# Undilated keys turned on VectorE instead of TensorE, with the pairs of that group moved later

## The reference

```python
for l in range(DEPTH):
    y = mixer_sublayer(x, ...)            # below
    x = layer_norm(alpha * x + y, ln_g[l], ln_b[l])

(aq, ak, av, ag, su, sv, sg, mq, mk, mv, mo, mg, mi, mf) = split_columns(x @ w_in)
aq = apply_partial_rope(aq, cos, sin); ak = apply_partial_rope(ak, cos, sin)
for gi, (window, dilation) in enumerate(ATT_GROUPS):   # (128, 1), (512, 4), (2048, 16)
    o, lse = dilated_window_attention(aq[gi], ak[gi], av[gi], window, dilation)
att = softmax over the groups' lse, applied to their o
...                                       # sgu, mLSTM with gates mi, mf
mix = concatenate([att * silu(ag), sgu * silu(sg), ml * silu(mg)])
return mix @ w_out
```

## Time and profile before

| | us |
|---|---|
| median of 3 runs | 1279.9 |
| the profiled execution, its own time | 1278.3 |
| its span, first to last instruction | 1276.6 |
| TensorE matmul busy | 1260.4 (99%) |
| VectorE busy | 896.2 (70%) |
| ScalarE busy | 694.4 (54%) |
| GpSimd busy | 248.0 (19%) |

### The profile page before, as it was taken

How to read it: one execution, slowest core, us unless ns; L and a number is a source line. 1 busy time by engine, 2 the same in 40 slices (tenths; PEclk the granted TensorE clock), 3 DMA queues, 4 the chain that set the end, 5 groups by cost and what they waited for, 6 DMA issues and landing times.

```text
span 1276.6 us, 16392 instructions
## 1 busy us (share of the span) xinstructions
PE 1260.4 (99%) x6358; PEld 1041.7 (82%) x6358; DVE 896.2 (70%) x1229; ACT 694.4 (54%) x959; POOL 248.0 (19%) x268
## 2 busy tenths in 40 slices
PE   9999999999999999999999999999999999999996
PEld 8888888888888888888888788887888888888885
DVE  5786876975667655865775769768756676567656
ACT  5477476555555544444564765666555655345441
POOL 0321522422320000400003223334131200004000
PEclk9999999999999999999999999999999999999998
DMA  9968758764665555466667587678546646555662
GB/s 334 316 200 262 235 189 271 263 200 140 204 200 171 188 185 183 155 224 194 201 199 224 190 271 232 210 251 278 184 133 217 191 153 214 165 188 198 190 208 89
DMA packets 129277, 264.97 MB, mean 208 GB/s; under 512 B 8824, under 2 KB 8976, under 8 KB 128688
## 3 DMA queue, kind: packets, MB, share of 16 engines
q1 hardware_dynamic: 123712, 247.23, 60.4%
q0 software_dynamic: 3680, 13.28, 3.0%
q10 hardware_dynamic: 1808, 3.42, 0.7%
HBM read 258.61 MB, written 5.28 MB: 207 GB/s over the span
## 4 chain that ended last, share of the span: by engine, by line
PE 92%; POOL 3%; DVE 2%; issue 2%; ACT 0%; DVEq 0%; POOLq 0%; ACTq 0%
PE ps L373 85%; PE ps L444 1%; PE ps L684 1%; DVE w_lo L1079 1%; DVE mix L1240 1%; PE ps L391 1%; PE ps L652 1%; POOL arena L1701 1%; PE ps L543 0%; POOL arena L1697 0%; PE ps L528 0%; PE ps L355 0%; PE ps L556 0%; POOL arena L1698 0%; PE ps L667 0%
## 5 line engine op out<-in xcount | busy, mean ns | idle before, releaser
L1079 DVE TENSOR_TENSOR w_lo<-w_raw,w_hi 128x1024 fp32r<-128x1024 f32 x408 | 529.3, 1315 | 321.2 <-ACT w_hi L749 319.8
L749 ACT ACTIVATE w_hi<-w_raw 128x1024 fp32r<-128x1024 f32 x408 | 428.3, 1058 | 404.2 <-PE ps L373 339.7
L373 PE MATMUL ps<-w_hi,xT_hi 128*128 128x512 f32 x1616 | 637.1, 394 | 4.5 <-DVE w_lo L1079 3.8
L373 PE MATMUL ps<-w_hi,xT_lo 128*128 128x512 f32 x1616 | 629.7, 390 | 0.0
L373 PE MATMUL ps<-w_lo,xT_hi 128*128 128x512 f32 x1616 | 629.2, 389 | 0.0
L373 PEld LDWEIGHTS ps<-w_hi,xT_hi 128*128 128x128 f32 x1616 | 303.4, 188 | 70.3 <-issue 7.4
L373 PEld LDWEIGHTS ps<-w_hi,xT_lo 128*128 128x128 f32 x1616 | 303.4, 188 | 63.9
L373 PEld LDWEIGHTS ps<-w_lo,xT_hi 128*128 128x128 f32 x1616 | 303.6, 188 | 61.2
L292 POOL TENSOR_TENSOR carried<-ident 1x1 f32<-1x1 f32 x30 | 17.6, 586 | 453.7 <-DVE arena L1433 178.7
L1240 DVE CUSTOM_DVE_ANT_0 mix<-xres,mix 128x1024 f32<-128x1024 f32 x64 | 88.4, 1381 | 1.1
L820 ACT ACTIVATE arena<-arena 32x256 f32<-32x256 f32 x128 | 53.2, 416 | 12.1 <-DVE arena L1156 10.5
(11 more groups left out here) (248 smaller groups left out, 847.2 us busy)
## 6 DMA issues: line engine op xcount, KB each, us to landing
w_raw<-w_in_dram SPq DMA_DIRECT2D x367, 512.0 KB, 4.5
w_raw<-w_out_dram SPq DMA_DIRECT2D x64, 512.0 KB, 4.8
mix<-gate_w_dram SPq DMA_DIRECT2D x32, 512.0 KB, 5.5
xres<-x_dram ACTq DMA_DIRECT2D x4, 512.0 KB, 8.9
v_dram<-arena POOLq DMA_DIRECT2D x4, 512.0 KB, 6.4
z<-v_dram POOLq DMA_DIRECT2D x8, 256.0 KB, 5.3
z<-ln_g_dram POOLq DMA_DIRECT2D x2, 1024.0 KB, 7.6
store<-ln_b_dram POOLq DMA_DIRECT2D x2, 1024.0 KB, 7.9
```

The source lines that it names most:

```text
L373: mm = pe.matmul(ps[2 * s + t][:], a[:, order[c] * KC + k, t * P:(t + 1) * P], b[:, k], start=(c + k + i == 0), stop=(c == CH - 1 and k == ...
L749: A(hi_of(n, c), w_raw[:, c % RING], ACT.Copy).then_inc(w_hi_done, 1)
L1079: TTn(lo_of(n, c), w_raw[:, c % RING], hi_of(n, c).bitcast(F32), ALU.subtract).then_inc(w_lo_done, 1)
```

## The change

The two copies `keys_copied` and TensorE's `key_transposes` go; the last group's keys take the path of the others, `turn(1)` on VectorE and `moved(1, ...)` on ScalarE. The scores of the first two pairs stand one chunk and a half or so later, behind the first chunk of the MO block instead of behind chunk 6 of the value block, and what follows them is moved likewise; the values of the last two pairs stand behind the first chunk of SU. On VectorE the gate pieces stand between remainders, in all three groups. The diff without the two removed copy functions and without the parts that only repeat such shifts:

```diff
 TensorE, last group
-                    def key_transposes():
-                        pe.wait_ge(roped, qk + 2)
-                        ...
-                                tr = pe.transpose(ps[6 + m // 2][:, at:at + P], z[:, 1, t, m * P:(m + 1) * P], ident[:])
-                        tr.then_inc(qk_ps, 1)
                     def scores(p):
                         if p == 0:
                             pe.wait_ge(qkT_act, qk + 2)
-                            pe.wait_ge(qkT_dve, l + 1)
+                            pe.wait_ge(comp_og_act, comp)
+                            pe.wait_ge(comp_og_dve, comp)
 ...
-                    chunks(n0 + 2, q0 + 2, 1, 0, 5)
-                    key_transposes()
-                    chunks(n0 + 2, q0 + 2, 1, 5, 7)
+                    chunks(n0 + 2, q0 + 2, 1, 0, CH)
+                    chunks(n0 + 3, q0 + 3, 0, 0, 1)
                     scores(0)
                     scores(1)
-                    chunks(n0 + 2, q0 + 2, 1, 7, 8)
-                    chunks(n0 + 3, q0 + 3, 0, 0, 1)
+                    chunks(n0 + 3, q0 + 3, 0, 1, 3)
                     prob_transposes(0)
-                    chunks(n0 + 3, q0 + 3, 0, 1, 2)
+                    chunks(n0 + 3, q0 + 3, 0, 3, 4)
                     prob_transposes(1)
-                    chunks(n0 + 3, q0 + 3, 0, 2, 3)
+                    chunks(n0 + 3, q0 + 3, 0, 4, 5)
 ...
                     for p in range(2):
                         values(p)
                     for p in range(2, PAIRS):
                         scores(p)
-                    chunks(n0 + 3, q0 + 3, 0, 3, 5)
+                    chunks(n0 + 3, q0 + 3, 0, 5, 7)
                     prob_transposes(2)
-                    chunks(n0 + 3, q0 + 3, 0, 5, 6)
+                    chunks(n0 + 3, q0 + 3, 0, 7, 8)
                     prob_transposes(3)
-                    chunks(n0 + 3, q0 + 3, 0, 6, 7)
-                    for p in range(2, PAIRS):
-                        values(p)
-                    chunks(n0 + 3, q0 + 3, 0, 7, 8)
 ...
-                chunks(N_SU, Q_SU, 0, 0, CH)
+                chunks(N_SU, Q_SU, 0, 0, 1)
+                for p in range(2, PAIRS):
+                    values(p)
+                chunks(N_SU, Q_SU, 0, 1, CH)
 ScalarE, last group
+                    split(n0 + 3, 0, 1)
+                    moved(1, 0, 8)
+                    split(n0 + 3, 1, 2)
+                    moved(1, 8, 16)
+                    split(n0 + 3, 2, 3)
 ...
-                    keys_copied()
-                    split(n0 + 3, 0, 3)
+                    take(n0 + 3, 1, vA[:, 0, :])
+                    split(n0 + 3, 3, 5)
                     exponentials(0)
-                    split(n0 + 3, 3, 4)
-                    take(n0 + 3, 1, vA[:, 0, :])
+                    split(n0 + 3, 5, 6)
                     exponentials(1)
                     prob_copy(0)
-                    split(n0 + 3, 4, 6)
+                    split(n0 + 3, 6, 8)
                     prob_copy(1)
 ...
                     prob_copy(2)
-                    split(n0 + 4, 0, 1)
+                    split(n0 + 4, 2, 3)
+                    take(N_SU, 0, mix[:, 0, 2 * BW:3 * BW])
                     prob_copy(3)
 VectorE, every group
-                    gate_sums(1)
-                    split(n0 + 2, 0, 4)
+                    split(n0 + 2, 0, 1)
+                    for i in pieces(g, 1):
+                        gate_piece_sums(i)
+                        c = i - pieces(g, 1)[0] + 1
+                        split(n0 + 2, c, c + 1)
+                    split(n0 + 2, 3, 4)
                     take(n0 + 2, 0, z[:, 1, 1, :])
-                    gate_sums(2)
-                    split(n0 + 2, 4, 8)
+                    for i in pieces(g, 2):
+                        gate_piece_sums(i)
+                        c = i - pieces(g, 2)[0] + 4
+                        split(n0 + 2, c, c + 1)
+                    split(n0 + 2, 6, 8)
+                    turn(1)
 VectorE, last group
-                    keys_copied()
-                    split(n0 + 3, 0, 2)
+                    split(n0 + 3, 0, 3)
                     ...
+                    take(n0 + 3, 1, vA[:, 1, :])
+                    split(n0 + 3, 3, 4)
                     score_maxima(0)
                     score_maxima(1)
 ...
                     prob_copy(2)
-                    split(n0 + 4, 0, 1)
+                    split(n0 + 4, 2, 3)
+                    take(N_SU, 0, mix[:, 1, 2 * BW:3 * BW])
                     prob_copy(3)
```

More of the change, by code:

```diff
@@ L811, in moved @@
                     def moved(which, first, last):
-                        act.wait_ge(turned, l * (2 * GROUPS - 1) + g * 2 + which + 1)
+                        act.wait_ge(turned, qk + which + 1)
                         for i in range(first, last):
@@ L891, in _ @@
                     split(n0 + 2, 4, 8)
-                    if g < NCOMP:
[L893 to L897, removed]
+                    split(n0 + 3, 0, 1)
[3 more added lines that the diff above has]
+                    split(n0 + 3, 2, 3)
+                    if g < NCOMP:
                         take(n0 + 3, 1, vS[:, 0])
@@ L906, in _ @@
                         continue
-                    keys_copied()
-                    split(n0 + 3, 0, 3)
+                    take(n0 + 3, 1, vA[:, 0, :])
+                    split(n0 + 3, 3, 5)
                     exponentials(0)
-                    split(n0 + 3, 3, 4)
-                    take(n0 + 3, 1, vA[:, 0, :])
+                    split(n0 + 3, 5, 6)
                     exponentials(1)
                     prob_copy(0)
-                    split(n0 + 3, 4, 6)
+                    split(n0 + 3, 6, 8)
                     prob_copy(1)
-                    split(n0 + 3, 6, 7)
+                    split(n0 + 4, 0, 1)
                     exponentials(2)
                     output_copy(0)
-                    split(n0 + 3, 7, 8)
                     exponentials(3)
                     output_copy(1)
+                    split(n0 + 4, 1, 2)
                     prob_copy(2)
-                    split(n0 + 4, 0, 1)
+                    split(n0 + 4, 2, 3)
+                    take(N_SU, 0, mix[:, 0, 2 * BW:3 * BW])
                     prob_copy(3)
-                    split(n0 + 4, 1, 3)
+                    split(n0 + 4, 3, 5)
                     output_copy(2)
                     output_copy(3)
-                    take(N_SU, 0, mix[:, 0, 2 * BW:3 * BW])
-                    split(n0 + 4, 3, 5)
                     act.wait_ge(mdiff_done, l * GROUPS + g + 1)
@@ L1158, in turn @@
                         f.then_inc(turned, 1)
-                    def keys_copied():
-                        dve.wait_ge(qk_ps, l + 1)
-                        V.tensor_copy(kT[:, 2:4, :], ps[7][:].rearrange("p (m t) -> p m t", m=2)).then_inc(qkT_dve, 1)
                     def comp_maxima():
@@ L1303, in _ @@
                     turn(0)
-                    gate_sums(1)
-                    split(n0 + 2, 0, 4)
-                    take(n0 + 2, 0, z[:, 1, 1, :])
-                    gate_sums(2)
-                    split(n0 + 2, 4, 8)
+                    split(n0 + 2, 0, 1)
[4 more added lines that the diff above has]
+                    split(n0 + 2, 3, 4)
+                    take(n0 + 2, 0, z[:, 1, 1, :])
+                    for i in pieces(g, 2):
[4 more added lines that the diff above has]
+                    turn(1)
                     if g < NCOMP:
-                        turn(1)
                         split(n0 + 3, 0, 3)
@@ L1325, in _ @@
                         TTn(gate_sum[:], gate_acc[:, :, 0, :], gate_acc[:, :, 1, :], ALU.add).then_inc(gates_summed, 1)
+                    take(n0 + 3, 1, vA[:, 1, :])
+                    split(n0 + 3, 3, 4)
                     score_maxima(0)
                     score_maxima(1)
-                    split(n0 + 3, 2, 4)
-                    take(n0 + 3, 1, vA[:, 1, :])
+                    split(n0 + 3, 4, 6)
                     prob_copy(0)
-                    split(n0 + 3, 4, 6)
+                    split(n0 + 3, 6, 8)
                     prob_copy(1)
-                    split(n0 + 3, 6, 7)
+                    split(n0 + 4, 0, 1)
                     score_maxima(2)
@@ L1354, in _ @@
                 split(N_SU, 4, 5)
+                output_copy(2)
+                output_copy(3)
                 split(N_SU, 5, 6)
```

3 lines of the change are left out of this document (removed).

## The result

The changed kernel takes 1271.65 us (median of 5 runs, 1271.05 to 1272.8), the kernel before on the same chip 1279.59 us (1277.83 to 1280.5). The ratio is 0.9944, 95% interval 0.9933 to 0.9955: **faster by 0.56%, some 7 us**. I had forecast 4.2 us less, 1275.7, in a range from 1274.3 to 1279.0. The direction was right; the gain is larger than the range allows. Profile against profile (1278.3 and 1271.65 us) it is 6.7 us, all of it in the span (1276.6 to 1269.9). The forecast missed by 4.05 us: 2.5 us are missing from its sum of 4.2, and 1.6 us come from setting that sum against a median that lay 1.6 us above the profiled execution.

The account below looks back on a forecast made before the run. TensorE, busy 1260.4 of 1276.6 us, was taken to bound the kernel. Terms -1.70 - 1.76 + 0.17 + 0.1 - 1.02 = -4.2 us, taken from a median of 1279.9, gave 1275.7 us; range 1274.3 to 1279.0.

Parts of the forecast that it names:

- The third, 2.1 us: Third of TensorE's three waits behind VectorE's remainders, 2.1 us; said to lie outside the last group and to stay.
- (a): Gate pieces between remainders, all groups: two TensorE stalls before the last groups' value blocks go, -1.70 us.
- (b): Eight key transposes leave TensorE in each layer's last group, 0.88 us each time: -1.76 us.
- (c): VectorE's turn and ScalarE's 16 moves of the keys: in time for layer 0's scores, +0.17 us stall in layer 1.
- M: The time when ScalarE's moves of the last group's keys end: forecast 276.5 in layer 0, 909.5 in layer 1.
- (d): After the scores: first exponentials end about when TensorE reaches the first probability transposes; +0.1 us, for layer 1.
- (e): Before SU's first chunk: the last pair's probability transposes fill TensorE's wait for PSUM copies, -1.02 us for both layers.
- (f): VectorE and ScalarE lose the two copies of the keys out of PSUM; booked at nothing.
- A: Rival: the wait moves to the scores, as the key turn takes 2.10 us; sum -2.8, 1277.1 us; chance 0.22.
- B: Rival: no room further on either, in VectorE's and ScalarE's queues; sum -0.6, 1279.3 us, no change; chance 0.13.
- C: Rival: late MO weights hold ScalarE's queue and the key moves; slower, +1.0, 1280.9 us; chance 0.07.
- D: Rival: the last transposes' new place before SU gains nothing, copy waits for its remainder; -3.2, 1276.7; 0.58 with the forecast.

Follow-up runs that it names:

- one old place: Changed kernel with the old order of gate pieces and remainders in the first group of layer 1 alone: 1274.11 us, ratio 0.9962 to the kernel before.
- the changed kernel once more: The changed kernel itself, unedited, measured again on the same chip as the best version: 1272.11 us, ratio 0.9940 to the kernel before.
- two remainders between the gate pieces: Changed kernel with VectorE's second run of gate pieces as G 4 5 G 6 7 instead of G 4 G 5 6 7: 1271.3 us, ratio 0.9935.
- the end of the last group: Changed kernel with the last pair's probability transposes back ahead of chunk 7 of the MO block: 1273.06 us, ratio 0.9955.
- gate pieces in the last group only: Changed kernel with gate pieces between remainders in the last group only, old order in the other groups: 1275.17 us, ratio 0.9969.
- everything but the gate pieces: Changed kernel with the gate pieces put back ahead of the remainders in all groups: 1276.11 us, ratio 0.9977 to the kernel before.

## Why the prediction was wrong, step by step

- **What bounds the kernel: right as a principle, wrong in one sentence.** "The third, 2.1 us, is none of the last group's, and the change leaves it" is the step that failed. I had looked where the last group is, found two of three waits, and taken the third for part of the start of layer 1 without its row. The edit (a) is in all three groups, and the third wait is a value block's first chunk as the other two are. It went when the gate pieces alone were moved and came back whenever they stood in the old order there (2.12, 2.13 and 2.13 us in three runs). Missing: -1.4 us net. The same step hid the three slow first chunks, -0.7 us, which are in no list of waits. With 0.26 us of the first 28 us and 0.1 of the last groups these are the 2.5 us missing from the sum.
- **(a) The two stalls of the last groups**: forecast -1.70, measured -0.88 and -1.30 by the starts of the matmuls, -2.18. A wait costs 0.24 us more than its bracket says: the bracket begins at the modelled end of the last matmul, 0.16 us after the next could have started (0.39 less 0.227), and the first step behind it takes 0.30 us instead of 0.227. "No remainder comes later" was right. Chunk 5 was named as next late, and was, in the one group that I did not walk.
- **(b) -0.88 us a layer**: right, shown by putting them back (+1.8 us for both). By the about 275 ns for one in the Trainium skill ("TensorE: Matmul & The Clock Gate", Part 4: PE-mode transpose) it would have been an estimated 2.2 us a layer. The trace agrees with that figure for one transpose by itself (mean 272 ns over these 16), and the runs go against adding it up for transposes in a row.
- **(c) The wait at the scores**: forecast 0 and 0.17 us, measured 0.53 and 0.02. My walk for the moves' end in layer 0 was 276.5, and they ended at 276.27. TensorE was there at 275.8 instead of 276.9: 0.72 us of this was won in the groups ahead, and 0.36 us my walk had too long, as it began at the edge of the bracket and took 2.75 us a chunk, where twelve steps of 0.227 us make 2.72. The turn took 1.23 us against a forecast of 1.25; the 311 ns for a 128x128 tile in the Trainium skill ("VectorE: DVE Perf Modes", The three transpose paths) would be an estimated 2.49 us for the eight and is not what the trace shows. That the place of the pairs, two chunks later than before, is just enough was right: one chunk earlier costs 4.6 us. And "M hangs on VectorE's turn of the queries, not on TensorE" was right. Five profiles have the same order between that turn and the scores of layer 0:

| profile | turn of the queries starts | moves end | last matmul to scores |
|---|---|---|---|
| the changed kernel | 244.91 | 276.27 | 0.85 |
| one old place | 244.85 | 276.19 | 0.80 |
| the changed kernel once more | 244.70 | 276.05 | 0.68 |
| two remainders between the gate pieces | 244.45 | 275.79 | 0.35 |
| the end of the last group | 244.18 | 275.53 | 0.32 |

From turn to end it is 31.34 to 31.36 us in all five, and TensorE could have begun within 0.1 us of 275.8 in all five. The turn itself waits each time for GpSimd's rotation of the queries, as in the changed kernel:

```profile
244.91 1.25 DVE L1133 STREAM_TRANSPOSE arena<-z 128x1024 f32<-128x1024 f32 x1 [1.71 <-POOL z L1634]
```

So what the scores lose is set by when GpSimd ends. What makes that differ between executions is not shown.

- **(d) First probability transposes**: forecast 0.1 in layer 1, measured 0.28 and 0.27 in the two layers. The chain from the moves to the end of the first exponentials was walked right (M+7.3 forecast; 283.69 - 276.27 = 7.4 us), the room was not: TensorE could have begun at M+7.2, where I had M+7.4.
- **(e) The end**: forecast -0.51 a layer, measured -0.78. Putting prob_transposes(3) back ahead of chunk 7 took 0.65 us of it away. The other 0.13 us I put down to one interruption of the chunks fewer, which that experiment kept; no run takes it alone.
- **(f) The two copies fewer**: forecast 0. No wait of TensorE points at it; no run tests it alone.
- **The own sum against the runs.** I subtracted 4.2 us from a median 1.6 us above the profiled execution, as if that 1.6 us would stay. It did not: the changed kernel's median is that of its profiled execution. The likely reason is that executions of the kernel before had the clock's drop behind the 2.1 us wait (1.6 us in a profile that has it), and that the drop went with the wait. For the three runs behind that median no clock is on record, so this part is argued, not shown.
- The rivals: A's wait came, in layer 0 only and at 0.53 us; B and C did not, and neither did D, as (e) gained more than forecast.

## What to carry to other kernels

Before summing a change, list every place in the program at which its edit acts, and put each wait of the bounding engine beside its instruction in the code; a wait left unplaced is not a wait left alone. Where a long side job stands in one queue with short work that the bounding engine needs, put the short work first, and walk each link again with the bounding engine earlier by what was won, for the slack behind it shrinks by just that. Set a sum that was read from one profile against the time of that execution, not against a median of others. Compare start distances, not only waits: work that arrives at the last moment costs without one.

## What the runs showed of the hardware

After an idle of TensorE of 2.13 us its granted clock fell to the lower level, 1.2 of 2.4 GHz, for about 3 us in two profiles (gate pieces in the last group only, one old place), and did not in two others with the same idle (the kernel before, everything but the gate pieces). It cost 1.6 us each time: eight or so matmuls at 0.43 us instead of 0.227, granted clock 0.50. No wait of 0.4 to 1.1 us in these groups had it behind it, nor had those of 2.89 and 2.56 us in the one profile that has them. On one and the same chip it goes with run times in groups: 11 runs of the kernel before with a median of 1278.2 us at 0.997 to 0.998, and 4 with one of 1280.2 us at 0.996.
